# Turning the squared-ReLU activations of both MLPs by 32x32 blocks on VectorE and quarter copies on ScalarE

## The reference

```python
c_act = jax.nn.silu(c)
for i in range(DEPTH):                                   # DEPTH = 2
    mod = (c_act @ w_ada[i] + b_ada[i])[:, None, :]      # w_ada[i]: 2048 x 12288
    sh_a, sc_a, g_a, sh_m, sc_m, g_m = jnp.split(mod, 6, axis=-1)
    h = x * (1.0 + sc_a) + sh_a
    y = diff_attention(h, ...) if i % 2 == 0 else sliding_window_attention(h, ...)
    x = layer_norm(ALPHA * x + (1.0 + g_a) * y, ln_mix_g[i], ln_mix_b[i])
    h = x * (1.0 + sc_m) + sh_m
    y = jnp.square(jax.nn.relu(h @ w_up[i])) @ w_down[i] # 2048 -> 8192 -> 2048
    x = layer_norm(ALPHA * x + (1.0 + g_m) * y, ln_mlp_g[i], ln_mlp_b[i])
```

## Time and profile before

| | |
|---|---|
| median of 3 runs | 2238.28 us (2237.4 to 2239.04) |
| the profiled execution's own time | 2239.4 us |
| its span from first to last instruction | 2237.6 us |
| TensorE busy | 2177.0 us (97%) |
| VectorE busy | 1679.1 us (75%) |
| ScalarE busy | 980.4 us (44%) |
| mean granted TensorE clock | 0.993 |
| HBM read | 592.60 MB, mean 266 GB/s |

### The profile page before, as it was taken

The page is one execution under the profiler, slowest core; times in us unless marked ns, Lnnn a source line. Parts: engine busy times, 40 slices in busy tenths (PEclk is TensorE's granted clock), DMA queues, the critical chain, the costliest instruction groups (busy, mean ns, idle before and its releaser), DMA issues.

```text
span 2237.6 us, 26038 instructions
## 1 busy us (share of the span) xinstructions
PE 2177.0 (97%) x10080; PEld 1805.1 (81%) x10080; DVE 1679.1 (75%) x1801; ACT 980.4 (44%) x1330; POOL 33.5 (1%) x53
## 2 busy tenths in 40 slices
PE   6999999999999999999999999999999999999997
PEld 6887888877888888888887787777888888888886
DVE  6899988887997797888786888676664555464557
ACT  1135544546433443443443655546433534343541
POOL 0001000000000000000000000000000000000000
PEclk9899999999999999999999999999999999999999
DMA  9989888877999999999986543366666666666673
GB/s 362 384 324 347 320 321 304 297 254 255 362 366 324 348 372 325 329 382 354 324 297 200 191 146 127 111 210 198 226 218 218 213 230 203 216 218 224 219 233 113
DMA packets 262591, 596.41 MB, mean 267 GB/s; under 512 B 13426, under 2 KB 14788, under 8 KB 262468
## 3 DMA queue, kind: packets, MB, share of 16 engines
q1 hardware_dynamic: 254800, 579.45, 74.0%
q10 hardware_dynamic: 7668, 15.30, 2.2%
HBM read 592.60 MB, written 2.10 MB: 266 GB/s over the span
## 4 chain that ended last, share of the span: by engine, by line
PE 88%; DVE 9%; issue 1%; ACT 1%; DMA 1%; ACTq 0%; DVEq 0%; POOL 0%; SPq 0%; POOLq 0%
PE pair L1641 25%; PE pair L1643 25%; PE pair L1642 25%; DVE acc L877 3%; DVE w_lo L862 2%; PE turn L1535 1%; PE pair L1899 1%; PE pair L1901 1%; PE pair L1900 1%; PE pair L1661 1%; PE pair L1663 1%; PE pair L1662 1%; PE turn L1970 1%; PE turn L1951 1%; ACT work L638 1%
## 5 line engine op out<-in xcount | busy, mean ns | idle before, releaser
L862 DVE TENSOR_TENSOR w_lo<-raw,w_hi 128x1024 fp32r<-128x1024 f32 x712 | 852.2, 1220 | 238.1 <-ACT w_hi L505 232.4
L505 ACT ACTIVATE w_hi<-raw 128x1024 fp32r<-128x1024 f32 x712 | 727.1, 1058 | 624.4 <-PE pair L1643 298.1
L1641 PE MATMUL pair<-w_hi,h_hi 128*128 128x512 f32 x1456 | 580.9, 399 | 1.5 <-DVE w_lo L862 0.7
L1643 PE MATMUL pair<-w_hi,h_lo 128*128 128x512 f32 x1456 | 568.0, 390 | 0.0
L1642 PE MATMUL pair<-w_lo,h_hi 128*128 128x512 f32 x1456 | 567.0, 389 | 0.0
L1641 PE MATMUL pair<-w_hi,f_hi 128*128 128x512 f32 x1056 | 413.9, 392 | 0.1
L1643 PE MATMUL pair<-w_hi,f_lo 128*128 128x512 f32 x1056 | 411.1, 389 | 0.0
L1642 PE MATMUL pair<-w_lo,f_hi 128*128 128x512 f32 x1056 | 410.8, 389 | 0.0
L890 DVE SCALAR_TENSOR_TENSOR acc<-ada_w,cvec,acc 128x1024 f32<-128x1024 f32 x300 | 383.7, 1279 | 1.8 <-DVE x L1248 0.9
L1643 PEld LDWEIGHTS pair<-w_hi,h_lo 128*128 128x128 f32 x1456 | 273.2, 188 | 58.3
L1641 PEld LDWEIGHTS pair<-w_hi,h_hi 128*128 128x128 f32 x1456 | 273.5, 188 | 57.8 <-issue 2.3
(11 more groups left out here) (186 smaller groups left out, 1643.0 us busy)
## 6 DMA issues: line engine op xcount, KB each, us to landing
ada_w<-in_w_ada_dram SPq DMA_DIRECT2D x320, 512.0 KB, 6.1
raw<-in_w_up_dram SPq DMA_DIRECT2D x128, 1024.0 KB, 5.8
raw<-in_w_down_dram SPq DMA_DIRECT2D x128, 1024.0 KB, 5.2
raw<-in_a_w_qkv_dram SPq DMA_DIRECT2D x48, 1024.0 KB, 7.3
ada_f<-in_w_ada_dram SPq DMA_DIRECT2D x44, 512.0 KB, 11.5
raw<-in_b_w_qkv_dram SPq DMA_DIRECT2D x20, 1024.0 KB, 5.1
raw<-in_a_w_o_dram SPq DMA_DIRECT2D x16, 1024.0 KB, 6.9
raw<-in_b_w_o_dram SPq DMA_DIRECT2D x16, 1024.0 KB, 5.1
```

The lines of the kernel that those rows point to most:

```text
L505: act.activation(w_hi[:, (b.n * SUB + n) % SPLITS], raw[:, slot, k:k + 2], ACT.Copy).then_inc(hi_ready, 1)
L862: dve.tensor_tensor(w_lo[:, slot, k:k + 2], raw[:, slot, k:k + 2], w_hi[:, (b.n * SUB + n) % SPLITS].bitcast(F32), ALU.subtract).then_inc( ...
L1641: pe.matmul(o, hi[:, kt, at], w[:, k], start=kt == 0, stop=False)
L1643: mm = pe.matmul(o, lo[:, kt, at], w[:, k], start=False, stop=kt == KT - 1)
```

## The change

The eight TensorE transposes of each up block are taken out, in both MLPs. In their place:

- VectorE transposes `R` by 32x32 blocks, in one instruction over 128x1024, into the same PSUM tile `turn[:, 0]` (`up_turn`, behind split_lo of n = 2).
- A 32x32 block stays in its own group of 32 partitions. Sixteen ScalarE copies per up block move the data from group a of `turn` into group c of `RR`, 32 partitions by 256 elements each (`up_move`, eight behind n = 3 and eight behind n = 4). Copy number i has a = i // 4 and c = i % 4, so the group that is written changes with every copy.
- The two squares read `RR` in SBUF in place of `turn` in PSUM, and stand behind n = 5; the subtraction on VectorE stands behind n = 5 as well.
- The relu stands behind split_hi of n = 2, before it stood behind n = 1.

```diff
+ON_CHIP = (0, 1)
...
+        def up_rows(tile):
+            return tile.rearrange("p t n -> p (t n)")
+        def by_feature(rows, c):
+            return rows.rearrange("p (t m c e) -> p c t m e", t=NT, m=4, c=4)[:, c]
+        def by_token(rows, a):
+            return rows.rearrange("p (m t a q) -> p a t m q", m=4, t=NT, a=4)[:, a]
+        def rows32(tile, i):
+            return tile[32 * i:32 * i + 32]
...
+            def up_move(first, last):
+                def run():
+                    act.wait_ge(up_blocks, st.turned.n + 1)
+                    for i in range(first, last):
+                        a, c = i // 4, i % 4
+                        ins = act.activation(by_token(rows32(up_rows(RR), c), a),
+                                             by_feature(rows32(turn[:, 0], a), c), ACT.Copy)
+                    if last == 16:
+                        ins.then_inc(up_moved, 1)
+                return run
+
+            def up_square_there(j):
+                def run():
+                    st.turned.n += 1
+                    act.wait_ge(up_moved, st.turned.n)
+                    wait(act, f_ready, st.up.at())
+                    act.activation(SQ.rearrange("p t n -> p (t n)"), up_rows(RR), ACT.Square)
+                    act.activation(f_hi[:, 4 * j:4 * j + 4], chunk(RR), ACT.Square).then_inc(up_hi_ready, 1)
+                    st.up.n += 1
+                return run
...
+                    if layer in ON_CHIP:
+                        if i < 4:
+                            hk[3], hk[4], hk[5] = up_move(0, 8), up_move(8, 16), up_square_there(i)
+                        block_(before=up_relu if i < 4 else None, hooks=hk, at=2)
+                        continue
...
+            def up_turn(b, pp):
+                dve.wait_ge(evacuated, b + 3)
+                dve.transpose(turn[:, 0], up_rows(R)).then_inc(up_blocks, 1)
+
+            def up_rest(j):
+                def run():
+                    st.turned.n += 1
+                    dve.wait_ge(up_hi_ready, st.turned.n)
+                    dve.tensor_tensor(f_lo[:, 4 * j:4 * j + 4], chunk(SQ), f_hi[:, 4 * j:4 * j + 4].bitcast(F32),
+                                      ALU.subtract).then_inc(f_ready, 1)
+                return run
...
+                    if layer in ON_CHIP and i < 4:
+                        block_(before=up_turn, later=(5, up_rest(i)), ada=mlp_pieces(b, halves), hooks=hooks)
+                        continue
...
+            def chunk_left():
+                st.up.n += 1
...
-                        hooks[1] = turn_up_count
+                        hooks[1] = chunk_left if layer in ON_CHIP else turn_up_count
```

More of the change, by code:

```diff
@@ L57 @@
 MASKED = -1e30
+ON_CHIP = (0, 1)
 T0_FIRST = 2
-T0_B = T0_FIRST + 16 + 4 * QUARTERS
+T0_B = T0_FIRST + 16 + (0 if 0 in ON_CHIP else 4 * QUARTERS)
 CHUNKS = [(0, 0), (0, 1), (1, 0), (1, 1), (0, 2), (1, 2), (0, 3), (1, 3)]
@@ L137, in __init__ @@
         self.up = Count()
+        self.turned = Count()
         self.bc = [0, 0]
@@ L309, in trunk @@
         kv_bias_arrived = sem("kv_bias_arrived")
+        up_blocks = sem("up_blocks")
+        up_moved = sem("up_moved")
+        up_hi_ready = sem("up_hi_ready")
         def bank(c):
@@ L970, in block_ @@
                         beside(SUB * st.block.n + n)
-                    if later and n == 4:
-                        later()
+                    if later and n == later[0]:
+                        later[1]()
                     if hooks and n in hooks:
@@ L1407, in mlp @@
                         hooks[7] = affine(site, b)
+                    if layer in ON_CHIP and i < 4:
+                        block_(before=up_turn, later=(5, up_rest(i)), ada=mlp_pieces(b, halves), hooks=hooks)
+                        continue
                     block_(before=(down_last if last else down_add)(i - 4) if i >= 4 else None,
-                           later=up_lo(i) if i < 4 else None, ada=mlp_pieces(b, halves), hooks=hooks)
+                           later=(4, up_lo(i)) if i < 4 else None, ada=mlp_pieces(b, halves), hooks=hooks)
             mlp(0, 1, 0)
```

## The result

The changed kernel takes 2257.1 us (median of 4 runs, 2255.15 to 2259.67), the kernel before 2238.64 (2237.4 to 2239.04). The ratio is 1.0084, 95% interval 1.0068 to 1.01: slower by 0.8%, 18.5 us. The forecast was 2256. The profiled execution took 2255.15 us, with a span of 2253.3.

What follows compares the result with a forecast made beforehand. TensorE, busy 97% of the span, was taken as the bound. First MLP +29.6 and second -12.4 us, transfers zero, sum to +17.2 on 2239.4 profiled, 2256.6; forecast median 2256 us, range 2241 to 2273.

Steps and rivals of the forecast that it cites:

- TensorE's gain: Removing eight TensorE transposes saves 0.90 us per up block, 14.4 us in each MLP, 28.8 us in all.
- The copies: Sixteen ScalarE copies per up block lose overlap when the partition group changes: 0.28 us, then fifteen at 0.41, 6.4 us.
- The transpose: VectorE's 128x1024 transpose in each up block takes 1.22 us, bounds 0.6 to 2.44.
- rival of two passes: VectorE's transpose takes 2.44 us, making the kernel 56 us slower, 2294, or from 2275 with cheaper copies; chance 0.10.
- The rings: First-MLP up blocks: VectorE transpose, ScalarE copies and squares, VectorE's list to next transpose: 24.6 us, 27.3 with affine, against 21.76.
- The waits by quarter: In the first MLP TensorE waits 19.1 us in the first quarter and 8.3 in each other; MLP total +29.6 us.
- The waits in the profile: TensorE's `pair` matmuls listed as waiting behind VectorE's `w_lo` for some 40 to 45 us in the first MLP.
- The second MLP: The second MLP gains 14.4 us and loses some 2 us in sixteen blocks: -12.4 us.
- The edge: Second-MLP up blocks: subtile 6's low part ready at B + 16.4, wanted at B + 16.3 (B: block's end on TensorE).
- Transfers: A late VectorE delays ada loads and the weight loads queued behind them on SyncE: taken as zero, up to 8 us.
- overlapping copies: Rival: ScalarE's copies in up blocks overlap at 0.28 us each, making the kernel 18.7 us faster, 2220; chance 0.09.
- the whole gain: Rival: VectorE has room in the first MLP, so the full -28.8 us is gained; chance 0.02.

Runs made afterwards that it cites:

- Half the copies: Changed kernel with the second eight of the sixteen ScalarE copies left out in every up block (half the activations stale): 2218.1 us, ratio 0.9912 to the kernel before.
- both spread kernels: Changed kernel with copies four behind each of n = 3 to 6, squares and subtraction behind n = 7: 2218.41 us; also with affine in down blocks: 2210.04 us.
- the kernel with runs of four: Changed kernel with copies reading and writing the same partition group, four in a row (wrong blocks copied): 2229.21 us, ratio 0.9964 to the kernel before.
- the spread order and the affine moved: Changed kernel with copies four behind each of n = 3 to 6, squares and subtraction behind n = 7, layer-norm affine in down blocks: 2210.04 us, ratio 0.9876.
- the experiment on overlap: Two variants of the changed kernel: written group kept for four copies, read group alternating, 2255.21 us; both groups kept for four copies, wrong blocks copied, 2229.21 us.

## Why the prediction was right

By its steps:

- **TensorE's gain, 0.90 us per up block.** Half the copies and both spread kernels, in which the second MLP has no waits of this kind, have it 13.8 to 14.5 us shorter (forecast 14.4).
- **The copies.** Forecast 0.28 for the first and 0.41 us for the others, measured 0.386. The mechanism, lost overlap at a change of partition group, was read from two pairs of rows, and the kernel with runs of four bears it out; whether one changed group is enough stays open, as said above. The size was taken from copies of 64 partitions: fifteen copies were priced 0.02 us too high each and the first 0.11 too low, so the sixteen took 6.2 us in place of 6.4.
- **The transpose.** Forecast 1.22 us, measured 1.25 to 1.26 (`STREAM_TRANSPOSE`, 1246 to 1260 ns, 32 times). One pass. The rival of two passes is out.
- **The rings.** Forecast 27.3 us with the affine: transposes start at 523.33, 550.40, 577.48 and 604.55, 27.07 apart. Forecast 24.6 without: 24.37 from 719.04 to 743.41, and again to 767.78. With a modulation sum, forecast 1.3 us more: 25.72 (767.78 to 793.50).
- **The waits by quarter.** Relu to relu of the first quarter grew from 180.44 to 195.86 us. With the 3.6 us that TensorE saves in four blocks, it lost 19.0 (forecast 19.1). The others by the same reckoning: 8.5, 8.0 and 7.1 (forecast 8.3 each). Two errors cancel in this: the rings were forecast 0.2 us too long, and each start of TensorE after a wait costs about 0.11 us that I had not counted (below).
- **The waits in the profile.** Here a sign of the prediction did not come: 40 to 45 us of waits were to be listed behind `w_lo` in the first MLP, and 31.9 are. The time lost is 42.7 us all the same (19.0 + 8.5 + 8.0 + 7.1). A matmul is listed with 0.39 us and the next one normally starts 0.23 us after it, so a listed wait is 0.16 us shorter than the delay, and the slow start adds 0.11. In these rows of TensorE the listed wait is 1.62 us, and the loss is 546.22 - 543.87 - 2 x 0.23 = 1.89 us:

```profile
543.87 0.39 PE L1711 MATMUL pair<-w_hi,h_lo 128*128 128x512 f32 x1
545.88 0.50 PE L1709 MATMUL pair<-w_hi,h_hi 128*128 128x512 f32 x1 [1.62 <-DVE w_lo L913]
546.22 0.39 PE L1710 MATMUL pair<-w_lo,h_hi 128*128 128x512 f32 x1
```

  With 0.27 us more for each of 29 waits, 31.9 becomes 39.7. Most of what is left are delays too short to be listed, like that at 1748.97 below. This is also, for the most part, why TensorE's busy time fell by only 15.4 us where 28.8 us of its work were taken out.
- **The second MLP.** Forecast -12.4, measured -10.0 us. The edge was there, at subtile 6 as said. Its low part ended just as it was wanted, and the block became 22.02 us (1732.72 to 1754.74) in place of 21.76. The forecast had 0.1 us for this and not 0.26. This term was mis-sized by 2.4 us, and most of it is the start after a wait. The first MLP came out 1.3 us below its forecast (28.3 for 29.6), so that of the 2.4 us only 1.1 show in the sum; that the median was met within 1.1 us is in part luck. TensorE's timeline there:

```profile
1748.61 0.39 PE L1711 MATMUL pair<-w_hi,h_lo 128*128 128x512 f32 x1
1748.97 0.50 PE L1709 MATMUL pair<-w_hi,h_hi 128*128 128x512 f32 x1
1749.31 0.40 PE L1710 MATMUL pair<-w_lo,h_hi 128*128 128x512 f32 x1
```

- **Transfers.** Taken as zero, with up to 8 us above. ScalarE's waits for weights did grow (from 119.4 + 54.6 = 174 us to 232 in the first MLP), but the sum left no room for a cost of them, and half the copies removed most of the loss with the same transfers and waits as long.

Of the rivals, overlapping copies is refuted by the 0.386 us and "the whole gain" by the waits. The second was a statement about this order of the instructions: with the spread order and the affine moved, nearly the whole gain is there. The first would not have come true in another order either, as long as the right blocks are moved (see the experiment on overlap). The prediction's working for it has a slip: the prices that it names make a ring 15 x 0.13 + 0.15 = 2.1 us shorter, not 2.25; its first quarter would then wait 10.7 us in place of 10.1, and its 2220 would be 2221.

## What to carry to other kernels

Work that is taken from the busiest engine and given to two half-idle ones that work in turns is not free because they are half idle. Add up the ring: from the instruction that waits, through the other engine's stretch, back through the first engine's own list. If it is longer than the period, it is the new bound, whatever the busy shares are (here 27.1 and 24.4 against 21.8 us, with VectorE busy for 76% of the span and ScalarE for 52%). The remedy is in the order: small pieces, each followed by something that lets the other engine go on.

## What the runs showed of the hardware that was not expected

- Copies of 32x256 on ScalarE overlap by about 0.11 us (0.27 us apart at 0.36 to 0.38 us duration) as long as both input and output begin in the same partition group as those of the one before. In the orders in which the input's or the output's group changed with every copy, they were 0.386 us apart. For short instructions this adds some 40% to their cost. Rows of the profile had told it for a change of both groups; that a change of the input's alone is enough fits the runs, but they do not rule out that the crossing of groups costs it.
- A 128x512 matmul after a wait of TensorE for `w_lo` is listed with 0.50 us where it otherwise has 0.39, and the next one starts 0.34 us later in place of 0.23 (545.88 to 546.22, 1748.97 to 1749.31). Thus such a wait costs about 0.11 us more than the delay of the first matmul, the shortest one too, and 0.27 us more than the profile lists for it.
- A 128x1024 float32 transpose by 32x32 blocks from SBUF to PSUM takes VectorE 1.25 to 1.26 us, as much as its other instructions of that size (1.22 to 1.29).
